# Storing the high and low halves of the weights word by word in one tile, on 256-byte boundaries

## The reference, cut to what matters

```python
z, xbc, dt_raw, q, f, v, g = _split(t @ w_in, IN_SIZES)          # first block, 1024 -> 7712 features
concatenate([ys, os_]) @ w_out                                    # 2048 -> 1024
v, gate = jnp.split(t @ w_up, 2, axis=-1)                         # 1024 -> 5632, three FFNs in all
gate = dwconv2d(gate, conv_w, conv_b, rows, cols)
return (jax.nn.gelu(gate, approximate=False) * v) @ w_down        # 2816 -> 1024
a, gate = jnp.split(t @ w1 + b1, 2, axis=-1)                      # conformer, 1024 -> 2048, then w2
proj = h @ w_in[l]                                                # second block, 1024 -> 3218
...
```

## The kernel before, in words

| stage | moving activations | stationary weights | after the change |
|---|---|---|---|
| `f`, `q` (h0, f_w, q_w) | 128 | 128 | 0, 0 |
| FFN 0 and 1, up | ffn_x: 0 | pre: 128; ffn_w: 0 | 0, 0 |
| FFN 0 and 1, down | ffn_h: 0 | pre: 128; ffn_down_w: 0 | 0, 0 |
| conformer in | conf_x: 0 | pre: 128; conf_w: 0 | 0, 0 |
| `projections` (h2) | 128 | pre: 128; pj_w: 0 | 0, 0 |
| FFN 2, up | ffn_x: 128 | pre: 128; ffn_w: 128 | 0, 0 |
| FFN 2, down | ffn_h: 0 | pre: 128; ffn_down_w: 128 | 0, 0 |

## Time and profile before

### The profile page before, as it was taken

One profiled execution on the slowest core, in us unless ns is written; L12 is line 12 of the kernel. 1 busy time (PEld: TensorE's weight loads), 2 busy tenths in 40 slices (PEclk: granted clock), 3 DMA queues, 4 the chain that ended last, 5 costly groups with the idle time before them and its releaser, 6 DMA issues. The chain is left out here.

```text
span 2826.2 us, 41654 instructions
## 1 busy us (share of the span) xinstructions
PE 2643.6 (94%) x16080; PEld 2040.3 (72%) x16080; DVE 1644.6 (58%) x2595; ACT 1090.9 (39%) x1805; POOL 161.7 (6%) x170
## 2 busy tenths in 40 slices
PE   6978899988889999999998999999899998999998
PEld 3753598876668788887664788888588765788876
DVE  3526412257766587853898688853763676544432
ACT  3441211136563455521524455522321254355421
POOL 0005300013213000000000000000000000000000
PEclk9989999999999999999999999999999998999999
DMA  8734312211114133241111233331431000233241
GB/s 306 246 108 145 124 46 60 59 43 40 43 44 131 46 109 91 87 123 47 55 49 34 68 107 94 96 113 52 124 91 45 3 17 28 86 96 96 82 119 61
DMA packets 382116, 240.93 MB, mean 85 GB/s; under 512 B 7825, under 2 KB 353809, under 8 KB 381969
## 3 DMA queue, kind: packets, MB, share of 16 engines
q1 hardware_dynamic: 381968, 238.89, 28.1%
HBM read 236.24 MB, written 2.10 MB: 84 GB/s over the span
## 5 line engine op out<-in xcount | busy, mean ns | idle before, releaser
L1164 DVE SCALAR_TENSOR_TENSOR ffn_acc<-ffn_pad,cols_sb,ffn_acc 128x512 f32<-128x512 f32 x380 | 263.6, 745 | 31.2 <-ACT ffn_acc L1091 31.1
L249 PE MATMUL bank<-ffn_x_high,pre_high 128*128 128x512 f32 x528 | 209.4, 397 | 4.9 <-DVE ffn_x_low L480 3.8
L251 PE MATMUL bank<-ffn_x_high,pre_low 128*128 128x512 f32 x528 | 207.3, 393 | 0.0
L250 PE MATMUL bank<-ffn_x_low,pre_high 128*128 128x512 f32 x528 | 207.3, 393 | 0.0
L251 PE MATMUL bank<-ffn_x_high,ffn_w_low 128*128 128x512 f32 x528 | 205.5, 389 | 0.0
L249 PE MATMUL bank<-ffn_x_high,ffn_w_high 128*128 128x512 f32 x528 | 205.5, 389 | 0.0
L250 PE MATMUL bank<-ffn_x_low,ffn_w_high 128*128 128x512 f32 x528 | 205.4, 389 | 0.0
L249 PE MATMUL bank<-ffn_h_high,ffn_down_w_high 128*128 128x512 f32 x480 | 188.7, 393 | 0.0
L251 PE MATMUL bank<-ffn_h_high,ffn_down_w_low 128*128 128x512 f32 x480 | 187.7, 391 | 0.0
L250 PE MATMUL bank<-ffn_h_low,ffn_down_w_high 128*128 128x512 f32 x480 | 187.6, 391 | 0.0
L754 ACT ACTIVATE ffn_down_w_high<-ffn_down_ring 128x1408 fp32r<-128x1408 f32 (+1 forms) x45 | 60.5, 1344 | 207.1 <-PE bank L251 175.7
(11 more groups left out here) (732 smaller groups left out, 6237.8 us busy)
## 6 DMA issues: line engine op xcount, KB each, us to landing
ada_ring<-in_ada_w SPq DMA_DIRECT2D x48, 1024.0 KB, 7.0
pre_ring<-in_ffn_w_up SPq DMA_DIRECT2D x88, 512.0 KB, 3.7
pre_ring<-in_ffn_w_in SPq DMA_DIRECT2D x44, 512.0 KB, 3.7
ffn_down_ring<-in_ffn_w_down SPq DMA_DIRECT2D x28, 704.0 KB, 4.5
pj_ring<-in_w_in SPq DMA_DIRECT2D x24, 512.0 KB, 3.5
ffn_down_ring<-in_ffn_w_out SPq DMA_DIRECT2D x14, 704.0 KB, 4.4
pre_ring<-in_conf_w SPq DMA_DIRECT2D x18, 512.0 KB, 4.8
f_ring<-in_mix_w_in SPq DMA_DIRECT2D x32, 256.0 KB, 3.2
```

The source lines that it names most:

```text
L249: pe.matmul(bank, weights[0], acts[0], start=start, stop=False)
L250: pe.matmul(bank, weights[0], acts[1], start=False, stop=False)
L251: return pe.matmul(bank, weights[1], acts[0], start=False, stop=stop)
L1164: dve.scalar_tensor_tensor(out=dst, in0=src, scalar=conv_w(2 * i + j, n), in1=dst, op0=ALU.mult, op1=ALU.add).then_inc(tapped[j], 1)
```

## The change

Every pair of stationary weight tiles becomes one tile with a last dimension of 2: word 0 of each pair is `high`, word 1 is `low`. `woven` hands out the two views, whose words lie 8 bytes apart. ScalarE and VectorE write the same elements as before, now 8 bytes apart, and LDWEIGHTS reads 128 words out of 1,024 bytes where it read 512. The moving activations stay in two dense tiles each. In `projections` a slot holds either pairs (`by_pair`) or two dense parts (`by_part`), by whether the weights are stationary or moving there. `LINE` becomes 256, so that every tile starts at a multiple of 256 bytes. The order, number and size of the instructions on every engine stay the same (6,596 rows for TensorE, 1,769 for VectorE, 998 for ScalarE, 141 for GpSimd and 201 for SyncE, the same row by row but for names of tiles and line numbers), and so do all waits.

```diff
-LINE = 128
+LINE = 256
+def woven(pairs):
+    return pairs[:, :, :, :, 0], pairs[:, :, :, :, 1]
...
-        self.pre_high = self.in_arena("pre_high", [P, 2, DT, P], F32R, 2 * slab)
-        self.pre_low = self.in_arena("pre_low", [P, 2, DT, P], F32R, 4 * slab)
+        self.pre_high, self.pre_low = woven(self.in_arena("pre_pairs", [P, 2, DT, P, 2], F32R, 2 * slab))
...
+    @contextmanager
+    def woven_room(self, **shapes):
+        self.rooms += 1
+        n = self.rooms
+        with ExitStack() as ctx:
+            yield [woven(ctx.enter_context(self.nc.sbuf_tensor(f"{name}_pairs_{n}", [*shape, 2], F32R, align_bytes=LINE)))
+                   for name, shape in shapes.items()]
...
-            core.split_room(**{f"{name}_w": [P, slots, kt, P]}) as ((high, low),), core.stage(*names, *extra) as (block, *sems):
+            core.woven_room(**{f"{name}_w": [P, slots, kt, P]}) as ((high, low),), core.stage(*names, *extra) as (block, *sems):
...
-            core.split_room(**{f"{name}_w": [P, slots - ready, per, P]}) as (own_w,), core.stage(*names) as (block, *sems):
+            core.woven_room(**{f"{name}_w": [P, slots - ready, per, P]}) as (own_w,), core.stage(*names) as (block, *sems):
...
-        with core.split_room(**{f"{name}_x": [P, DT, SEQ], f"{name}_w": [P, 2, DT, P]}) as (parts, (high, low)):
+        with core.split_room(**{f"{name}_x": [P, DT, SEQ]}) as (parts,), core.woven_room(**{f"{name}_w": [P, 2, DT, P]}) as ((high, low),):
...
+        by_pair = pj_w[:].rearrange("p s (k f n) -> p s k f n", k=DT, n=2)
+        by_part = pj_w[:].rearrange("p s (n k f) -> p s n k f", n=2, k=DT)
...
+            if TOKENS_AT <= s < MOBA_AT or s >= LAST_AT:
+                return by_part[:, slot(s), 0], by_part[:, slot(s), 1]
+            return by_pair[:, slot(s), :, :, 0], by_pair[:, slot(s), :, :, 1]
```

More of the change, by code:

```diff
@@ L1227, in conformer_gate @@
              "summed", "mean_done", "square_done", "var_done", "root_done", "inverted", "eps_in", "next_in", "next_high"]
-    with core.split_room(conf_x=[P, DT, SEQ], conf_w=[P, 2, DT, P]) as (parts, (high, low)), \
+    with core.split_room(conf_x=[P, DT, SEQ]) as (parts,), core.woven_room(conf_w=[P, 2, DT, P]) as ((high, low),), \
             core.room(conf_pad=[P, pads, width], conf_sig=[P, 2, SEQ], conf_diag=[P, 2, most, P], conf_sq=[P, 2, SEQ],
@@ L1646, in entry @@
                    entry_form=[P, 2, SEQ]) as (ctx, pad, w_ring, ada_rows, form), \
-            core.split_room(xbc_w=[P, 2, DT, P]) as ((high, low),), core.stage(*names) as (block, *sems):
+            core.woven_room(xbc_w=[P, 2, DT, P]) as ((high, low),), core.stage(*names) as (block, *sems):
         (cols_in, const_in, rows_in, x_in0, x_in1, ctx_in, piece_in0, piece_in1, piece_in2, slab_in0, slab_in1, steps_in,
@@ L2461, in room @@
         with self.core.room(gate_ring=[P, 2, *part[1:]]) as (self.ring,), \
-                self.core.split_room(gate_w=[P, self.slots, *part[1:]]) as ((self.high, self.low),):
+                self.core.woven_room(gate_w=[P, self.slots, *part[1:]]) as ((self.high, self.low),):
             yield
@@ L3006, in gla @@
         o_gates = core.nc.alloc_sbuf_tensor_at("o_gates", [P, DT, SEQ], F32, offset=f_at)
-        mix = [core.nc.alloc_sbuf_tensor_at(f"mix_first_{n}", [P, 2, DT, P], F32R, offset=f_at + DT * SEQ * 4 + 2 * DT * P * 4 * n)
-               for n in range(2)]
+        mix = woven(core.nc.alloc_sbuf_tensor_at("mix_pairs", [P, 2, DT, P, 2], F32R, offset=f_at + DT * SEQ * 4))
         stream = GateStream(core, w_in[:, MIX_AT["z"]:MIX_AT["xbc"]], w_in[:, MIX_AT["g"]:], h, y, o_gates, var, mix, w_out)
@@ L3587, in projections @@
     flat = cs[:].rearrange("p h t k -> p (h t) k")
-    with core.room(pj_ring=[P, SLOTS, DT, P]) as (ring,), core.split_room(pj_w=[P, SLOTS, DT, P]) as ((high, low),), \
+    with core.room(pj_ring=[P, SLOTS, DT, P]) as (ring,), core.some_parts(pj_w=[P, SLOTS, DT * P * 2]) as (pj_w,), \
             core.stage("slab_in0", "slab_in1", "slab_in2", "small_in", "w1_in", "high_done", "low_done", "job_done", "evicted", "cleared",
@@ L3603, in projections, with slab_parts @@
         n_small = 6
+        by_pair = pj_w[:].rearrange("p s (k f n) -> p s k f n", k=DT, n=2)
+        by_part = pj_w[:].rearrange("p s (n k f) -> p s n k f", n=2, k=DT)
         def slot(s):
             return (s - PREPARED) % SLOTS
+        def slab_parts(s):
+            if s < PREPARED:
+                return core.pre_high[:, s], core.pre_low[:, s]
+            if TOKENS_AT <= s < MOBA_AT or s >= LAST_AT:
+                return by_part[:, slot(s), 0], by_part[:, slot(s), 1]
+            return by_pair[:, slot(s), :, :, 0], by_pair[:, slot(s), :, :, 1]
         @block.sync
@@ L3647, in part @@
             def part(s, k):
-                if s < PREPARED:
-                    return [core.pre_high[:, s, k, :], core.pre_low[:, s, k, :]]
-                return [high[:, slot(s), k, :], low[:, slot(s), k, :]]
+                return [half[:, k, :] for half in slab_parts(s)]
             def ready(s, k):
@@ L3676, in tokens @@
                         ready(s + SLOTS - 1, k)
-                    pe.matmul(target, h[0][:, k, tok], high[:, some, k, :], start=(k == 0), stop=False)
-                    pe.matmul(target, h[0][:, k, tok], low[:, some, k, :], start=False, stop=False)
-                    mm = pe.matmul(target, h[1][:, k, tok], high[:, some, k, :], start=False, stop=(k == DT - 1))
+                    high, low = by_part[:, some, 0, k, :], by_part[:, some, 1, k, :]
+                    pe.matmul(target, h[0][:, k, tok], high, start=(k == 0), stop=False)
+                    pe.matmul(target, h[0][:, k, tok], low, start=False, stop=False)
+                    mm = pe.matmul(target, h[1][:, k, tok], high, start=False, stop=(k == DT - 1))
                 mm.then_inc(job_done, 1)
@@ L4019, in _ @@
                 for part in range(2):
-                    split_half(dve, ring[:, slot(s)], high[:, slot(s)], low[:, slot(s)], part, 2 * n + part, high_done, low_done)
+                    split_half(dve, ring[:, slot(s)], *slab_parts(s), part, 2 * n + part, high_done, low_done)
                 beside(s)
```

## The result

The changed kernel takes **2860.47 us** (median of 4, 2855.49 to 2863.32) against 2832.11 us for the kernel before (median of 4): ratio 1.0102, 95% interval 1.0087 to 1.0118. It is 28 us slower; 2820 us had been predicted. Three executions on record (3805.35 us of the kernel before, 6175.39 us with the alignment alone, 6834.12 us with the FFNs' weights half off) were in a slow state and are left out of every ratio and median here. The profiled execution has a span of 2856.5 us, 30.3 more than the 2826.2 of before.

What follows compares the result with a forecast made beforehand. TensorE, busy for 94% of the span with a train of float32r matmuls, was taken as the bound. Alignment saves 13.4 us and interleaving costs 0: 2833.45 - 13.4 + 0 = 2820 us, range 2768 to 2872.

Steps and rivals of the forecast that it cites:

- Part 1: All starts at multiples of 256 bytes: 2,304 matmuls in TensorE-bound stages gain 5.8 ns each, 13.4 us.
- The FFN terms: FFN 0 and 1 `pre` weights (1,056 matmuls), FFN 2 down (480), first down-projection pairs (144), gaining 5.8 ns each.
- Part 2: Weight words 8 bytes apart: claimed to leave the step at 226.7 ns, so no gain or loss.
- the bounds given: Step with interleaved weights: 214.6 ns from half a plain float32 matmul, 238.3 from 226.7 plus 2 x 5.8.
- the surplus of 13.4 ns: Step of 226.7 ns over 213.3 for 512 columns at 2.4 GHz; claimed to be the stream's own, whatever loads beside.
- (a): With 32 weight and 256 moving columns a step takes 113.5 ns, so the surplus follows moving columns, not weight columns.
- (b): Last matmul of `q`, no load beside, takes 388 ns like the dense 389; without the surplus about 376.
- (c): At granted clock 0.50 steps take 430 ns where 512 columns take 427: at half the pace the stream keeps up.
- The writers at nothing: ScalarE and VectorE writing words 8 bytes apart cost nothing; even doubled `high` copies leave ScalarE at 188 of 247 us.
- walking in step keeps collisions alive: Every load of 6,960 matmuls: interleaved loads stay in the stream's way, 2860 us, or 2901 at twice that; together 0.28.
- The first rival: In 6,960 TensorE-bound matmuls the surplus is a collision that interleaving ends: 97 us less, 2736 us; chance 0.15.
- A load at half rate: Loads of 213 ns and more show only in the `f` gates' 384 steps: 36 us, 2856 us; within 0.28 together.

Runs made afterwards that it cites:

- the FFNs' weights half off: Changed kernel with high and low in 128-word blocks, only the FFNs' own weights moved by 128 bytes: 2828.17 us, ratio 0.9989 to the kernel before.
- the probes: Three kernels without the model, only trains of 48 float32r matmuls with varied weight starts, spacings and columns; read by step (226.7 ns dense in step), not total time.
- the two kernels with blocks: Changed kernel with 128 words of high, then 128 of low: with LINE 256 ratio 0.9917 (repeat 0.9911), with LINE 128 0.9988, to the kernel before.
- the second probe: Model left out, 25 named trains of 48 matmuls: 226.7 ns a step dense in step, 233.3 woven in step, 215.8 with the stream all in one word.

## Why the prediction was wrong, step by step

- *What bounds the kernel, and the step as the measure*: right. TensorE's busy time grew by what the span grew (30.2 and 30.3 us), and 24-step readings tell the change of the FFNs, which is 22.4 of it.
- *The relative start modulo 256 bytes is what makes 226.7 or 232.5*: right, shown in both directions (alignment alone, half off alone) and by the probes.
- *Part 1, 13.4 us*: mechanism right, size low. Alone it gave 19 us (0.9932), or 22 between the two kernels with blocks. The FFN terms came out near the counts (8.3 for 9.7 us), the conformer's not at all (0 for 1.1). Not in the sum were 0.5 us of the `tokens` matmuls and what `projections` and the attention behind them gained with a higher granted clock, in both comparisons. Why TensorE was granted more there is not shown. Over all executions of the two kernels with blocks the mean granted clock was 0.971 with the new starts and 0.972 with the old ones, no higher, so what the excess is in the executions without a trace stays open. In the changed kernel the gain of part 1 is absent but for a little of this (-1.5 and -2.7 us).
- *Part 2, "Interleaved weights would leave that alone. ... I take 226.7"*: **this is the step that failed**. It measured 233.3, inside the bounds given (214.6 to 238.3) but at neither its middle nor its chosen value. The price is 6.6 ns for each of the 4,656 matmuls that were in step, and 0.8 for the 2,304 that were at 232.5 already: 30.7 + 1.8 = 32.6 us, against 28 us in the medians. In the three FFNs, where the clock was full, the same prices give 21.6 us and the traces show 22.4.
- *How it failed*: the conclusion that the surplus of 13.4 ns is the stream's own was right for 10.9 of them (215.8 ns with one word of stream). It was then taken to mean that loads do not matter. But 226.7 was the time with loads that are dense and in step, not the time of a stream left in peace, and the earlier trace rows already showed that a load can add 5.8 ns. A new address pattern of the load had to be treated like a new start: as likely out of step as in.
- *The three reasons for it*: (a), 113.5 ns with 32 columns, was the case of 256 moving columns; with 512 the probe has 231.7 for 32 columns, more than for 128, so it could not stand for the load's share. Nor is such a load a quarter as long: 109 ns for 32 columns and 188 for 128 in the second probe. (b), the last matmul without a load beside, doesn't show the load's share: the last of `q` in the changed kernel, with no load beside it either, takes 397 ns where the one ahead of it, with a load, has 394. (c), at half the clock, fits both views: in the changed kernel's `f` gates, while the granted clock was 0.50, six steps with woven weights take 2.56 us, 426.7 ns each, so at that clock neither the surplus nor the price of weaving shows.

```profile
417.46 0.63 PE L262 MATMUL bank<-h_high,f_w_pairs 128*128 128x512 f32 x1
...
420.02 0.63 PE L262 MATMUL bank<-h_high,f_w_pairs 128*128 128x512 f32 x1
...
L264 PE MATMUL bank<-h_high,q_w_pairs 128*128 128x512 f32 x1 | 0.4, 397 | 0.0
L263 PE MATMUL bank<-h_low,q_w_pairs 128*128 128x512 f32 x1 | 0.4, 394 | 0.0
```

- *The writers at nothing*: right. ScalarE's interleaved copies cost 8%, far from the doubling that the prediction allowed for, VectorE's nothing, and both stayed hidden.
- *The rivals*: "walking in step keeps collisions alive" had the right place, size and time (2860 us, at a chance of 0.28), and the sign that was named for it, steps above 226.7 in FFN 2's up projection. That it met 2860 to the microsecond is luck: it took 5.8 ns a step for what measured 6.6, and nothing for the 0.8 and for the clock. Its picture fits only in part. The pace it assumed is about right: a load takes (188 - 109) / 96 = 0.82 ns a column, 4.9 bytes per ns, and the stream 2,048 bytes in 226.7 ns, 9.0 bytes per ns. But woven loads are slow at all starts, and fastest 64 bytes off. The first rival, an end to the surplus, is out: nothing with a real stream came below 226.7. A load at half rate is out too: the `f` gates' matmuls of 256 columns, and those of the probe, keep 120 ns with woven weights.
- *The recurrence*: 8.0 of the 30.3 us lie there in the profiled execution, and I first took them for a consequence of woven gates. That fell: the same stretch at half clock appears in executions with dense gates and not in every one. The totals at half clock from 300 us on are the same in the two profiled executions (121.4 and 121.5 us), so the clock adds next to nothing to the comparison as a whole.

What stays open: why a dense load in step, and only it, leaves the stream at 226.7; the probes give the pattern, not its cause.

## What to carry to other kernels

Where float32r matmuls of 512 columns follow each other without a gap, read the start-to-start step and not the busy share, and compare it between stages with different tile starts: here equal starts modulo 256 bytes for moving and stationary tiles, with adjacent words, were worth 19 to 22 us of 2833 for one constant, some 11 or 12 of them in the steps themselves. Keep the weights' words adjacent, however convenient interleaving is. And when a row gives the cost of an operation beside another, it holds for that pair of access patterns; before a pattern changes in 7,000 places, 48 matmuls of it in a probe tell the price of a step.

## What the runs showed of the hardware that had not been expected

- A float32r matmul of 512 columns: 215.8 ns when the stream is one word, 226.7 with dense loads of 128 columns in step, 229 or more in every other arrangement tried; 32 or one word to load make it no faster. Plain float32 (429.2) reacts neither to weaving nor to a start half off, and 256 columns of float32r (120.0) not to weaving.
- Float32r matmuls of 384 columns, with the weights as the stream: 173.4 to 173.5 ns a step in the eight traces with `LINE` at 256, 175.9 to 176.0 in the three with 128.
- What a train pays can depend on how it began: woven weights have 233.3 ns a step by themselves and 235.5 behind matmuls of 256 columns.
- ScalarE writing words 8 bytes apart: 8% longer (1053 to 1135 ns for 1024 elements); VectorE: nothing (1220 to 1224).
- TensorE was granted 0.50 (1.2 GHz) for 17 us, busy throughout, in one execution and 2.4 GHz at the same place in another of the same kernel (the two executions with blocks), after the same 55.4 busy of 61 us.
